# Attention masks of a fused transformer block: from matrix products to a masked maximum on VectorE

## The reference, cut to what matters

```
s = einsum(q, kc) * scale;  p_cmp = masked_softmax(s, cmp_end <= t)        # 63 compressed blocks
s = einsum(q, k_sel) * scale;  p = masked_softmax(s, pos <= t)             # selected blocks
s = einsum(q, kw) * scale;  p = masked_softmax(s, kpos <= t and kpos > t - 512 and kpos >= 0)   # window
out = g0 * o_cmp + g1 * o_slc + g2 * o_win

def masked_softmax(s, mask):
    return softmax(where(mask, s, -1e30)) * mask
```

## Time and profile before

| | us |
|---|---|
| median of 3 runs | 1455.14 (1454.55 to 1455.33) |
| the profiled execution | 1455.89 |
| its span | 1453.7 |
| PE, PEld busy | 1419.3 (98%), 1215.5 (84%) |
| DVE, ACT, POOL busy | 871.0 (60%), 622.7 (43%), 161.5 (11%) |
| granted TensorE clock, mean | 0.999 |

### The profile page before, as it was taken

One profiled execution on the slowest core, in us unless ns is written; L12 is line 12 of the kernel. 1 busy time (PEld: TensorE's weight loads), 2 busy tenths in 40 slices (PEclk: granted clock), 3 DMA queues, 4 the chain that ended last, 5 costly groups with the idle time before them and its releaser, 6 DMA issues.

```text
span 1453.7 us, 21619 instructions
## 1 busy us (share of the span) xinstructions
PE 1419.3 (98%) x7942; PEld 1215.5 (84%) x7950; DVE 871.0 (60%) x1630; ACT 622.7 (43%) x1235; POOL 161.5 (11%) x178
## 2 busy tenths in 40 slices
PE   7999999999999999998999999999999999999999
PEld 6888888887888888897988878888888788888887
DVE  3002682106766776669793596655566598579764
ACT  5013303216555545460440477655555554444441
POOL 2433333521000000000242000000000000000000
PEclk9999999999999999999999999999999999999999
DMA  5211114200000000012111015444445956643332
GB/s 178 59 51 51 44 36 131 73 0 8 1 2 1 1 1 2 1 45 116 30 51 36 30 65 182 150 149 141 155 158 169 333 174 214 203 127 94 101 110 87
DMA packets 78253, 129.41 MB, mean 89 GB/s; under 512 B 8973, under 2 KB 26826, under 8 KB 78154
## 3 DMA queue, kind: packets, MB, share of 16 engines
q1 hardware_dynamic: 77968, 128.01, 27.6%
q10 hardware_dynamic: 186, 0.08, 0.0%
HBM read 94.51 MB, written 33.55 MB: 88 GB/s over the span
## 4 chain that ended last, share of the span: by engine, by line
PE 89%; DVE 7%; issue 2%; ACT 2%; DMA 1%; SPq 0%; DVEq 0%; ACTq 0%
PE ps L518 66%; PE ps L2105 6%; PE ps L2065 4%; PE ps L2080 4%; PE ps L2125 3%; PE ps L2049 1%; PE ps L1942 1%; PE ps L2099 1%; DVE hgrn_vg L1636 1%; PE ps L760 1%; DVE negmax L1495 1%; DMA x_in<-in_x_dram 1%; PE ps L2070 1%; PE ps L627 1%; DVE q_stack L1488 1%
## 5 line engine op out<-in xcount | busy, mean ns | idle before, releaser
L518 PE MATMUL ps<-mlp_w_low,hidden_high 128*128 128x512 f32 x448 | 174.4, 389 | 0.0
L518 PE MATMUL ps<-mlp_w_high,hidden_high 128*128 128x512 f32 x448 | 174.4, 389 | 0.0
L518 PE MATMUL ps<-mlp_w_high,hidden_low 128*128 128x512 f32 x448 | 174.4, 389 | 0.0
L518 PE MATMUL ps<-w_high,hT_high 128*128 128x512 f32 (+1 forms) x448 | 170.6, 381 | 0.8 <-ACT cmp_v L1072 0.7
L518 PE MATMUL ps<-w_high,hT_low 128*128 128x512 f32 (+1 forms) x448 | 168.3, 376 | 0.0
L518 PE MATMUL ps<-w_low,hT_high 128*128 128x512 f32 (+1 forms) x448 | 168.1, 375 | 0.0
L2105 PE MATMUL ps<-nsa,probs_T 128*128 128x64 f32 x1056 | 137.8, 274 | 0.0
L1298 ACT ACTIVATE mlp_w_high<-mlp_w_raw 128x512 fp32r<-128x512 f32 x112 | 70.6, 630 | 147.7 <-PE ps L518 147.7
L1667 DVE TENSOR_TENSOR mlp_w_low<-mlp_w_raw,mlp_w_high 128x512 fp32r<-128x512 f32 x112 | 76.9, 691 | 93.4 <-ACT mlp_w_high L1199 93.4
L2105 PEld LDWEIGHTS ps<-nsa,probs_T 128*128 128x128 f32 x1056 | 129.1, 193 | 0.0
L1747 DVE TENSOR_TENSOR mlp_w_low<-mlp_w_raw,mlp_w_high 128x512 fp32r<-128x512 f32 x112 | 77.2, 689 | 65.6 <-ACT mlp_w_high L1298 65.5
(11 more groups left out here) (233 smaller groups left out, 2846.3 us busy)
## 6 DMA issues: line engine op xcount, KB each, us to landing
hidden_raw<-hidden_pieces SPq DMA_DIRECT2D x112, 256.0 KB, 2.7
mlp_w_raw<-in_w_mlp_in_dram SPq DMA_DIRECT2D x32, 512.0 KB, 4.3
hidden_pieces<-hidden SPq DMA_DIRECT2D x64, 256.0 KB, 2.8
mlp_w_raw<-in_w_mlp_out_dram SPq DMA_DIRECT2D x64, 256.0 KB, 4.2
w_raw<-in_w_in_dram SPq DMA_DIRECT2D x56, 256.0 KB, 2.7
hidden_pieces<-hidden_s SPq DMA_DIRECT2D x48, 256.0 KB, 2.2
x_in<-in_x_dram SPq DMA_DIRECT2D x8, 512.0 KB, 7.6
w_raw<-in_w_out_dram SPq DMA_DIRECT2D x16, 256.0 KB, 2.8
```

The lines of the kernel that those rows point to most:

```text
L518: ins = nc.tensor.matmul(out_ap, a_hl[i], b_hl[j], start=first and n == 0, stop=last and n == 2, skip_group_check=onto_a_sum_already_read)
```

## The change: what it does

PE makes no mask product for slc and win items: an item is one or two pairs of products, and the last one signals `qk_done`. The mask tile becomes a row of masks in SBUF, 1792 columns of bf16 (448 KB in place of 96): the identity, zeros, the causal tile, the window's far tile, zeros, the causal tile again. A slice of it that is as wide as the item has the right tiles at the right columns. In `maximum(j)` the `tensor_reduce` is replaced by one `tensor_tensor_reduce`: it adds the slice to the scores, multiplies by -1, writes the result over the scores in PSUM, and takes the minimum along the row into negmax. ACT's exponential reads the negated scores with `scale=-1.0`. The cmp item is left as it is. The masks lie at another place in SBUF, behind cmp_diff. Cut to the core:

```diff
-    masks = np.zeros((P, 3 * P), np.float32)
+    masks = np.zeros((P, P + S + 5 * P), np.float32)
     masks[:, 0:P] = eye
-    masks[:, P:2 * P] = np.where(i[None, :] <= i[:, None], 0.0, NEG)
-    masks[:, 2 * P:] = np.where(i[None, :] > i[:, None], 0.0, NEG)
+    masks[:, S:P + S] = np.where(i[None, :] <= i[:, None], 0.0, NEG)
+    masks[:, P + S:2 * P + S] = np.where(i[None, :] > i[:, None], 0.0, NEG)
+    masks[:, 5 * P + S:] = np.where(i[None, :] <= i[:, None], 0.0, NEG)
...
-    masks = sb("masks", [P, 3 * P], BF16, 61440)
+    masks = sb("masks", [P, P + S + 5 * P], BF16, 83968)
...
-                act.activation(o, sv, ACT.Exp, bias=negmax[:, j % NEGMAX:j % NEGMAX + 1],
+                act.activation(o, sv, ACT.Exp, bias=negmax[:, j % NEGMAX:j % NEGMAX + 1], scale=-1.0,
...
                     sv = scores_view(j)
-                    dve.tensor_reduce(negmax[:, j % NEGMAX:j % NEGMAX + 1], sv, AX if len(sv.shape) == 2 else mybir.AxisListType.XY,
-                                      ALU.max, negate=True).then_inc(max_done, 1)
+                    w = len(tiles) * P
+                    mask = masks[:, P + S:P + S + w] if kind == "win" and t >= WIN_T else masks[:, P + S - w:P + S]
+                    if len(sv.shape) == 3:
+                        mask = mask.rearrange("p (a b) -> p a b", a=2)
+                    dve.tensor_tensor_reduce(sv, sv, mask, -1.0, 3.0e38, ALU.add, ALU.min, negmax[:, j % NEGMAX:j % NEGMAX + 1])\
+                        .then_inc(max_done, 1)
...
-                    for q, (c, k) in enumerate(mine):
-                        ins = nc.tensor.matmul(ps[:, banks[b], c:c + P], masks[:, 0:P], masks[:, k * P:(k + 1) * P],
-                                               start=False, stop=q == len(mine) - 1, skip_group_check=True)
```

More of the change, by code:

```diff
@@ L2056, in scores @@
                 nb = 1 if w <= BW else 2
[L2057 to L2060, removed]
                 for b in range(nb):
                     o = ps[:, banks[b], 0:w // nb]
-                    mine = [(c, k) for bb, c, k in ms if bb == b]
                     for n, k_ in enumerate((KS_H, KS_L)):
@@ L2067, in scores @@
                                                .rearrange("p a n -> p (a n)"),
-                                               start=n == 0, stop=n == 1 and not mine, skip_group_check=True)
-                    for q, (c, k) in enumerate(mine):
-                        ins = nc.tensor.matmul(ps[:, banks[b], c:c + P], masks[:, 0:P], masks[:, k * P:(k + 1) * P],
-                                               start=False, stop=q == len(mine) - 1, skip_group_check=True)
+                                               start=n == 0, stop=n == 1, skip_group_check=True)
                 ins.then_inc(qk_done, 1)
```

## The result

The changed kernel takes 1446.1 us (median of 6 runs, 1444.3 to 1448.5) against 1455.1 (1454.4 to 1456.3): a ratio of 0.994, 95% interval 0.993 to 0.995, or 9.0 us less. I had forecast 4.2 us less, with 1447.0 as the low end. The direction was right, the size was half of what came, and the time lies 0.9 us under the range. Only runs in the fast state are compared: one execution of the kernel before, in a later round, took 1954.0 us at a mean granted clock of 0.676 and is left out.

What follows compares the result with a forecast made beforehand. PE bounds most of a head, DVE and ACT the rest. Masks removed give -1.04 us and the masked maximum +0.52 per head, so -0.52, -4.2 us for 8 heads: 1450.9 against 1455.1, range 1447.0 to 1459.8.

Steps and rivals of the forecast that it cites:

- the map of a head: PE sets a head except before slc4's scores, from first stage transposes to PE's next transposes, and through the last exponential.
- The middle mask: Mask product between two key products on PE, 4 per head: removing each gains 0.13 us, two on PE's path.
- The final mask: Mask product ahead of the value products on PE, 16 per head: removing each gains about 0.065 us.
- win2's maximum: DVE maximum that idles 0.32 us behind its mask; without two final masks ahead it starts 0.13 us earlier per head.
- The masked maximum: DVE's two-instruction replacement for the plain maximum: adds d in four places of a head, 0.52 us per head.
- d: Added length of a DVE maximum, to negmax's signal and to the next DVE operation: 0.13 us, range 0.07 to 0.22.
- ScalarE's accumulator read: Existing row used to size the second DVE instruction: it lengthens its pair by 0.09 us, so 0.10 was taken.
- Half rate: Rival: each element of the masked maximum costs 1.04 ns more on DVE, 1474 to 1521 us, say 1490; chance 0.06.
- a slow instruction: Rival: masked maximum costs far more per instruction, deciding from d = 0.26; 1459.6 us at d = 0.40; chance 0.14.
- the rival that it gives nothing: Rival: value products start as late without masks, so PE gives nothing back and DVE's cost stays: 1459.3 us; chance 0.06.
- The rival that the gain of PE's long stretch goes into waits: Rival: the 0.585 us from slc4's scores to the first stage transposes is lost to later exponentials: 1455.6 us; chance 0.12.
- The masked maximum at no cost: Rival: the second DVE instruction disappears in the tail of the first, -8.3 us, 1446.8 us; chance 0.04.

Runs made afterwards that it cites:

- pe_alone: Changed kernel with the plain maximum back on VectorE and no scale on ScalarE, slc and win masks left out: 1445.2 us, 0.991 to 0.994 of before.
- dve_alone: Changed kernel with all 160 mask products kept on PE, so masks are added twice: 1457.8 us, 1.000 to 1.002 of before.
- keep_final: Changed kernel with the 128 final mask products back on PE: 1454.0 us, 0.998 to 1.000 of before.

## Why the prediction was half right

- **The bound and the map of a head** were right: PE for most of it, VectorE and ScalarE in three stretches. pe_alone and dve_alone have the signs of the two sides. In the first of the three stretches the two maxima cost one signal delay, not two.
- **The middle mask**, 0.13, was right. It was read between two places that differed in the mask alone, k_low to k_low.
- **The final mask** was the step that failed. I took 0.06 from one start to the next and said that "what follows does not show in the step". It did: the next value products were 0.06 later as well. The term is 0.12 instead of 0.065. My gain had 12 final masks in it, 10 on PE's path and two ahead of win2's maximum: 0.66 us per head more, 5.3 us, which is more than the miss of 4.8. keep_final measures 8.7 us for all final masks together. I had the means to see it, since the middle mask had already shown a product behind a mask that was slower.
- **The masked maximum** was mis-sized too, and in the same direction. d was 0.13 for queue and signal alike; it is 0.01 for the queue and 0.07 for the signal, and it counts three times per head and not four: 1.6 to 1.7 us in all where the forecast had 4.2, another 2.5 us. The 0.07 was the low end of my range, and the row nearest in kind, ScalarE's accumulator read, was a poor guide to the queue. The Trainium skill's 75 ns per instruction, which I set beside the sum (Vector Engine (DVE) Microarchitecture Reference, Measured stream behaviour on trn2), is a price in the queue. The accumulator read does not pay it there, where it costs 0.01; that the signal is late by 0.07 is another quantity of nearly the same size.
- **Given back.** With both terms as measured the forecast's sum would have been -1.04 - 0.66 + 0.21 = -1.49 per head; this head had -1.06 and the mean of the heads is -1.15. What was given back is 0.16 ahead of win2's maximum (a wait for VectorE's cmp operation), 0.17 in PE's stretch (0.13 of it slc5's wait for ScalarE) and 0.11 at slc7. The forecast took every mask on PE's path at its full price. So the miss is as small as 4.8 us by luck: the two mis-sized terms make 7.8, and about 3 went into waits that the sum did not have.
- **The rivals.** Half rate is out (1.03 ns per element), and so is a slow instruction (0.07 at most, where that rival begins at 0.26). PE gives back more than forecast (1.35 per head in pe_alone), so the rival that it gives nothing is out. The rival that the gain of PE's long stretch goes into waits was right in kind and wrong in size: 0.17 of 0.86. The masked maximum at no cost had the nearest time, 1446.8, but not for its reason.

## What to carry to other kernels

Measure what a matmul occupies over the whole group, from a landmark in front of it to one well behind it, and compare with the same group without it: the start of the next row alone missed half of the cost here. The small bf16 product with weights of its own between fp32 products was not paid by its columns (0.12 us for 128 or 256 of them). The accumulator read on VectorE delayed who waited for it by 0.07 and the queue by 0.01, so it was dear only where the chain passed. And once the chain leaves the bounding engine, look at what the other engine waits for in its in-order queue: moving 0.9 us of independent work into such a wait gave 8.1 us alone, nearly as much as the whole change (9.2), and 13.0 on top of it.

## What the runs showed of the hardware that I had not expected

- In front of key and value products a mask product of 256 columns costs PE the same as one of 128 (1.54 us for win4 with either), and a second one of 128 adds 0.055. In front of slc7's stage transposes 128 columns cost 0.07 and 256 cost 0.05 more.
- The accumulator read of VectorE (142 ns a row) overlaps the next operation: both start at 396.08, and a maximum takes 0.01 more of the queue than before.
- In some executions PE runs at half of its full clock, 1.2 instead of 2.4 GHz, for 3.4 or 6.8 us. The profiled execution of dve_alone had it in its first head and twice later, that of before early in the MLP. The stretch ahead of the fall and the fall itself in dve_alone, the first of the two in before, and then the fall of before in the MLP (length, busy us by engine, clock, DMA):

```profile
335.00:340.50 5.50, 4.05 (x36) 3.65 (x34) 4.77 (x13) 3.79 (x11) 1.84 (x2) 1.00 0.02 3
340.50:347.50 7.00, 7.00 (x33) 5.89 (x33) 3.52 (x14) 2.56 (x10) 0.00 (x0) 0.51 0.00 1
```

```profile
335.00:340.50 5.50, 4.06 (x36) 3.65 (x34) 4.65 (x10) 3.79 (x11) 1.82 (x2) 1.00 0.02 3
```

```profile
860.00:868.00 8.00, 6.77 (x23) 5.42 (x24) 7.89 (x13) 5.78 (x12) 0.00 (x0) 0.79 0.16 54
```

  Ahead of the fall in the first head PE is busy in 4.05 of 5.50 us, but the kernel before has the same gaps there and keeps the full clock, so what decides it stays open. In the changed kernel the place of the MLP's fall comes 9.6 us earlier (850.4 to 858.4), and its clock is 1.00 there. A fall costs 1.6 us in the MLP and nearly 3 in the first head (36.1 us from the first head's cmp products to the second's in dve_alone, 33.1 in before, with 0.2 of the difference for the masked maximum). This is why the head period is the sharper measure, and the runs of one kernel spread by 1.4 to 5.4 us.
